# The out-projection of an mLSTM block as seven block products instead of eight

## The chip, the cores and the metric

One core of a Trainium2 chip runs one transformer block. The metric is the device time of one launch in microseconds; the kernel before takes 1096.12 us (median of three runs, 1095.81 to 1096.61). VectorE is called DVE in the rows, ScalarE ACT, GpSimd POOL, TensorE PE, and SyncE, which issues most transfers, SP.

## The reference, cut to what matters

```python
def mlstm_mixer(h, w_in, b_if, norm_w, w_out):
    ...
    hc = rms_norm(from_chunks(hc)).reshape(bsz, seq, ML_V_WIDTH) * norm_w.astype(f32)   # 4 heads of 256
    out = hc * jax.nn.sigmoid(o.astype(f32))
    return out.astype(h.dtype) @ w_out          # 1024 x 1024 by 1024 x 1024

        x = x + g1 * y                          # y: the mixer's output
        h = rms_norm(x) * (1.0 + sc2) + sh2
        x = x + g2 * swiglu(h, ffn_w_gate_up[layer], ffn_w_down[layer])
```

Everything is float32. The change is in `out @ w_out`, in the adding of it to x, and in the second norm behind it.

## The kernel before, in words

The 1024 tokens are eight tiles of 128. Every float32 product is made of three products of a rounded part (H) and a residue (L): HH, HL, LH. So an operand is first rounded by ScalarE into hH or wH, and VectorE subtracts that from the source into hL or wL. Order between engines is by semaphores; each engine works its own queue in the order in which the code is written.

**Heads.** `head(h)` runs four times. For each of eight chunks c TensorE does `scores`, a projection of 24 matmuls and `attend(h, c - 1)`. VectorE does `weighted`, `value_low`, `state` (the matrix C, which `attend` reads), `divide`, `gating`, `weighted_low`, and in between two `ada_item` (the sums of the modulation rows, both operands in SBUF; SP loads one item for each, `ada_item` in the sync queue). GpSimd makes qs (qT times sI) for the next `attend`, and hg, the gated head output, 128x256 per head and chunk, row of tile t in `hg[:, t, :]`. In head 3 it also scales the first out-projection weights by the gate g1 (`scale_unit`, L714).

**Out-projection.** w_out comes in four units of 256 columns; g1 is multiplied in by GpSimd in the raw buffer, ScalarE rounds (`split_H`), VectorE takes the residue (`split_L`, L1289). There is one raw buffer of two halves: `load_unit` (L427) loads a half only when the residue of the half before it has been taken. Rows of hg are normed per head: `head_root` (L942, ScalarE) takes the root for four tiles of all heads, `head_rstd` the reciprocal, `head_norm` (L723 on GpSimd, L1423 on VectorE) multiplies a whole row tile of 128x1024. TensorE transposes each tile (`out_transposes`, L2098, two banks of PSUM); `og_high` (L948) rounds it out of PSUM into hH and `og_low` (L1430) takes the residue out of PSUM into hL. `y_tile(n)` on TensorE (L2223) makes 24 matmuls, eight K tiles times three, of 512 columns (two units) or 256; on VectorE (L1612) it adds the bank to x in x2. Tiles go over the first two units, then the last; the order is in `y_sequence` (L60).

**End of the stage.** `Y_SECOND` finishes one row tile after the other in the order of TOKENS. For each finished tile ScalarE squares and roots it (`row_square`, L1104), VectorE takes the reciprocal (`row_inverse`), scales it into xs (`norm_row`, L1846), TensorE transposes it in two halves into three banks (`transposes2`, L2009), ScalarE and VectorE copy one half each with the modulation (`copy_rows`, L1073 and L1854), ScalarE and VectorE split it (`high`, `low`, L1331). On VectorE the order in each step is add, residues of an earlier tile, copy, and only then reciprocal and `norm_row`. GpSimd makes sums of halves of x2 (T1 to T4) for the up products, which are already made as 2x2 block products with seven multiplications; `up_product(n, q)` (L2267) waits for the operand of its q in all tiles. The first of them are (0, 2), (0, 1), (1, 2), (1, 1), and then (0, 5), the first that reads T1.

## Time and profile before

| | |
|---|---|
| median of the runs | 1096.12 us |
| profiled execution, first to last instruction (span) | 1095.6 us |
| its own time as a run | not listed apart; the runs lie within 1095.81 to 1096.61 |
| TensorE, VectorE, ScalarE, GpSimd busy | 98%, 67%, 41%, 14% |
| TensorE's granted clock | 0.999 over the span |
| out-projection, first product to first up product | 355.87 to 459.58 us |

The span is 0.5 us under the median. Busy time is the time in which an engine executes; a row's "us" for a group of several instructions reaches from the first start to the last end. Successive instructions overlap in the rows by about a tenth of a microsecond, so the pitch (start to start) is shorter than the duration. "<-" behind idle time names what ended it.

### The profile page before, as it was taken

To read this page: it belongs to the slowest core of one execution; us is meant where nothing else is said; L and a number is where in the kernel's file an instruction comes from. 1 tells how busy PE (TensorE), PEld (TensorE's weight loads), DVE (VectorE), ACT (ScalarE), POOL (GpSimd) and SP (SyncE) were. 2 spreads that over 40 slices of the span, in tenths; PEclk is the share of its full clock that TensorE was granted. 3 is DMA by queue.
4 is the path that set the end of the run, shared out by engine and by line. 5 is a ranking of instruction groups with operands and counts; after the bars stand their busy time and mean duration, and the time that the engine had idled before them with its cause. 6 is when DMAs were issued, how large, how long until landed. Compare 5 with 4: busy or idle time off the path is not lost.

```text
span 1095.6 us, 14969 instructions
## 1 busy us (share of the span) xinstructions
PE 1077.3 (98%) x5290; PEld 910.4 (83%) x5290; DVE 729.4 (67%) x1285; ACT 450.8 (41%) x826; POOL 157.4 (14%) x145
## 2 busy tenths in 40 slices
PE   6999999999999999999999999999999999999997
PEld 6899888888888897888888888888888888888886
DVE  6867757477479636888767566766766465844676
ACT  7862322232224316664433343333333325544444
POOL 3732312212326412410000000000000000000000
PEclk9999999999999999999999999999999999999999
DMA  9425532432531523115555526444552889655643
GB/s 377 167 80 169 185 109 87 140 114 61 160 114 58 193 78 116 78 39 172 159 169 166 184 93 221 145 142 156 177 187 91 289 281 396 231 193 184 200 154 154
DMA packets 86970, 177.11 MB, mean 162 GB/s; under 512 B 8152, under 2 KB 31320, under 8 KB 85872
## 3 DMA queue, kind: packets, MB, share of 16 engines
q1 hardware_dynamic: 85984, 174.80, 47.1%
q0 software_dynamic: 480, 1.09, 0.4%
q8 instruction: 42, 0.69, 0.3%
q10 hardware_dynamic: 432, 0.27, 0.1%
q14 instruction: 32, 0.26, 0.1%
HBM read 135.97 MB, written 40.16 MB: 161 GB/s over the span
## 4 chain that ended last, share of the span: by engine, by line
PE 95%; DVE 2%; DMA 1%; ACT 1%; issue 1%; POOL 0%; DVEq 0%; POOLq 0%; SPq 0%
PE OP L2263 27%; PE OP L1994 19%; PE O L2263 15%; PE ST L2263 5%; PE DC L2263 5%; PE AD L2263 5%; PE O L1994 4%; PE ST L1994 4%; PE AD L1994 2%; PE DC L1994 1%; PE O L2141 1%; PE ST L2042 1%; PE O L2157 1%; PE DC L2157 1%; PE O L2042 1%
## 5 line engine op out<-in xcount | busy, mean ns | idle before, releaser
L1994 PE MATMUL OP<-wH,hH 128*128 128x512 f32 (+1 forms) x400 | 142.1, 355 | 0.4 <-issue 0.4
L1994 PE MATMUL OP<-wH,hL 128*128 128x512 f32 (+1 forms) x400 | 139.1, 348 | 0.0
L1994 PE MATMUL OP<-wL,hH 128*128 128x512 f32 (+1 forms) x400 | 138.7, 347 | 0.0
L1759 DVE TENSOR_TENSOR dL<-dF,dH 128x1024 fp32r<-128x1024 f32 x77 | 93.0, 1223 | 68.6 <-ACT dH L1159 67.7
L1159 ACT CAST dH<-dF 128x1024 fp32r<-128x1024 f32 x77 | 79.9, 1052 | 88.0 <-DMA dF<-w_units 36.2
L2263 PE MATMUL OP<-tH,wsH 128*128 128x512 f32 x264 | 102.7, 389 | 0.0
L2263 PE MATMUL OP<-tH,wsL 128*128 128x512 f32 x264 | 102.7, 389 | 0.0
L2263 PE MATMUL OP<-tL,wsH 128*128 128x512 f32 x264 | 102.7, 389 | 0.0
L1994 PEld LDWEIGHTS OP<-wH,hL 128*128 128x128 f32 x400 | 75.6, 189 | 9.6
L1994 PEld LDWEIGHTS OP<-wH,hH 128*128 128x128 f32 x400 | 75.7, 189 | 9.3 <-issue 0.8
L1994 PEld LDWEIGHTS OP<-wL,hH 128*128 128x128 f32 x400 | 75.8, 190 | 8.6
L1071 ACT CAST wsH<-wsF 128x512 fp32r<-128x512 f32 x88 | 53.2, 620 | 49.6 <-DVE wsF L1675 42.8
L1071 ACT CAST wsH<-raw 128x512 fp32r<-128x512 f32 x66 | 38.8, 619 | 75.5 <-DMA raw<-w_units 61.8
L2263 PE MATMUL O<-hH,wsL 128*128 128x512 f32 x176 | 68.5, 389 | 0.0
L2263 PE MATMUL O<-hH,wsH 128*128 128x512 f32 x176 | 68.5, 389 | 0.0
L2263 PE MATMUL O<-hL,wsH 128*128 128x512 f32 x176 | 68.5, 389 | 0.0
L1714 DVE TENSOR_TENSOR wsL<-wsF,wsH 128x512 fp32r<-128x512 f32 x88 | 58.2, 686 | 14.4 <-ACT wsH L1071 14.4
L1670 DVE TENSOR_TENSOR wsF<-raw 128x512 f32<-128x512 f32 x21 | 14.5, 691 | 74.7 <-DMA raw<-w_units 65.2
L768 POOL TENSOR_TENSOR hg<-hc,gate 128x256 f32<-128x256 f32 x32 | 34.6, 1080 | 164.5 <-DVE gate L1518 164.5
L2263 PEld LDWEIGHTS OP<-tH,wsL 128*128 128x128 f32 x264 | 49.6, 188 | 10.3
L2263 PEld LDWEIGHTS OP<-tH,wsH 128*128 128x128 f32 x264 | 49.6, 188 | 10.3
L2263 PEld LDWEIGHTS OP<-tL,wsH 128*128 128x128 f32 x264 | 49.5, 188 | 10.2
(331 smaller groups left out, 2601.0 us busy)
## 6 DMA issues: line engine op xcount, KB each, us to landing
raw<-w_units SPq DMA_DIRECT2D x76, 512.0 KB, 4.6
dF<-act_mid SPq DMA_DIRECT2D x77, 256.0 KB, 2.7
ada<-ada_rest SPq DMA_DIRECT2D x64, 256.0 KB, 3.0
wst<-w_units SPq DMA_DIRECT2D x44, 256.0 KB, 5.0
down_mid<-wst SPq DMA_DIRECT2D x22, 512.0 KB, 3.2
dF<-down_mid SPq DMA_DIRECT2D x44, 256.0 KB, 3.0
dF<-w_units SPq DMA_DIRECT2D x33, 256.0 KB, 5.2
ada<-ada_first SPq DMA_DIRECT2D x8, 1024.0 KB, 10.0
```

What stands on the lines that cost most here:

```text
L768: nc.gpsimd.tensor_tensor(hg[:, c - 1, h * DV:(h + 1) * DV], hc[:, (c - 1) % 2, :], gate[:, (c - 1) % 2, :], ALU.mult).then_inc(hg_ok, 1)
L1071: nc.scalar.copy(wsH[n % 2][W_SLOT.index(q)][:], src).then_inc(c_H, 1)
L1159: nc.scalar.copy(dH[g][:], dF[g][:]).then_inc(d_H, 1)
L1670: nc.vector.tensor_tensor(f[5][:], gate_up_block(0, 1), gate_up_block(1, 1), ALU.add).then_inc(c_sum, 1)
L1714: nc.vector.tensor_tensor(wsL[n % 2][i][:], src, wsH[n % 2][i][:].bitcast(F32), ALU.subtract).then_inc(c_L, 1)
L1759: nc.vector.tensor_tensor(dL[g][:], dF[g][:], dH[g][:].bitcast(F32), ALU.subtract).then_inc(d_L, 1)
L1994: ins = nc.tensor.matmul(out_ap, lhs[a], rhs[b], start=(n == 0 and i == 0), stop=(last and i == 2))
L2042: ins = nc.tensor.matmul(XT_BANKS[2 * (t % 2) + j][:, k * P:(k + 1) * P], xin[:, t, (4 * j + k) * P:(4 * j + k + 1) * P], diag[:, t % 2, : ...
L2141: nc.tensor.matmul(O[c % 2][:, 0:width], qs[:, c % 2, :], C[:, 0:width], start=True, stop=False)
L2157: ins = nc.tensor.matmul(out_ap, lhs[a], rhs[b], start=(first and i == 0), stop=(i == 2))
L2263: ins = nc.tensor.matmul(out_ap, lhs[a], rhs[b], start=(first and i == 0), stop=(last and i == 2), skip_group_check=True)
```

## The change

w_out is cut into a 2x2 matrix of 512x512 blocks, and so is the normed, transposed activation (A11, A12 the first four token tiles with heads 0 and 1 and heads 2 and 3, A21 and A22 the last four). Seven products q of a sum of activation blocks (T1 to T4, A11, A12, A22) with a sum of weight blocks give the result; each product has four token tiles r of 12 matmuls of 512 columns. The partial products stay in PSUM banks and are added to x by VectorE after each product.

- **Weight sums** (`out_weights`): in heads 1 and 2 SP loads the four blocks of w_out in eight chunks into the part of hg that head 3 will fill, GpSimd scales each chunk by g1 and makes four sums, SP saves them to a buffer in DRAM (`out_mid`) and later loads them as units. The load of g1 moves from head 3 to head 1.
- **Norm**: `head_root(0)` covers heads 0 and 1 and runs in head 2; `head_root(1)` covers heads 2 and 3. `head_norm` does half a row (128x512): heads 0 and 1 by GpSimd in head 3's chunks 0 to 3; of heads 2 and 3 tiles 0 and 1 by VectorE, the rest by GpSimd.
- **Transposes**: 16 half tiles; five of them inside head 3. ScalarE copies each back into hg (`og_copy`), GpSimd sums blocks (`og_sums`, 16 of 128x512), ScalarE rounds and VectorE takes residues out of SBUF (`og_high`, `og_low`, 28 each).
- **Weights**: seven units; two of them and the unit for q = 4 are scaled by GpSimd, the others come scaled.
- **End of the stage**: twelve products in the order of `Y_ENDS`; TOKENS changes; a finished tile's reciprocal and `norm_row` follow its add at once on VectorE; the transposes use two banks, and those of the last two tiles run behind up products. The x loads of tiles 0 to 3 no longer wait for the last modulation row.

The diff, cut to its core:

```diff
@@ plans
-TOKENS = (0, 1, 4, 2, 5, 3, 6, 7)
+TOKENS = (0, 1, 2, 4, 3, 5, 6, 7)
+OUT_SEQ = (1, 2, 6, 7, 4, 5, 3)
+    ends = [(4, 0), (4, 1), (5, 0), (4, 2), (5, 1), (3, 0), (4, 3), (3, 1), (5, 2), (5, 3), (3, 2), (3, 3)]
+    ends = {2: row_tiles(0), 3: row_tiles(1), 5: row_tiles(2), 7: row_tiles(3), 8: row_tiles(4), 10: row_tiles(5)}
+    after = {0: row_tiles(6), 1: row_tiles(7)}
@@ banks
-        Y_BANKS = [OP[0], OP[1], DC, AD]
+        OUT_X = [OP[0], OP[1], DC, O[1]]
+        OUT_P2 = [O[0], AD]
+        OUT_Y = [O[0], AD, DC, O[0]]
-        TR_BANKS = [ST[0], ST[1], O[1]]
+        TR_BANKS = [ST[0], ST[1]]
@@ SP, in head(h)
+            load_at = {(1, 6): (0, 1), (1, 13): (2,), (1, 15): (3,), (2, 3): (4,), (2, 5): (5,), (2, 9): (6,), (2, 11): (7,)}
+            save_at = {(1, 12): 0, (1, 14): 1, (2, 2): 2, (2, 4): 3, (2, 8): 4, (2, 10): 5, (2, 14): 6}
...
                     ada_item(h, i, first)
+                    if (h, i) in save_at:
+                        save_out_chunk(save_at[h, i])
+                    for n in load_at.get((h, i), ()):
+                        load_out_chunk(n)
@@ GpSimd
+            def out_weights(n):
...
+                nc.gpsimd.tensor_tensor(bv, bv, gv, ALU.mult).then_inc(so_sum, 1)
+                pool.wait_ge(so_sum, 5 * n + 1)
+                nc.gpsimd.tensor_tensor(b22, b12, b22, ALU.add).then_inc(so_sum, 1)
...
+            chunk_at = {(1, 4): 0, (1, 5): 1, (1, 7): 2, (2, 0): 3, (2, 2): 4, (2, 3): 5, (2, 5): 6, (2, 6): 7}
...
+            for r in range(3):
+                og_sums("T1", r)
+            head_norm(1, 2)
+            head_norm(1, 3)
+            og_sums("T1", 3)
+            for t in range(4, NT):
+                head_norm(1, t)
+            for r in range(4):
+                og_sums("T2", r)
...
+            for r in range(4):
+                og_sums("T3", r)
+            scale_unit(U_OUT + 4)
+            for r in range(4):
+                og_sums("T4", r)
@@ VectorE, behind the heads
+            og_low("A11", 3)
             divide(NH - 1, NT - 1)
             gating(NH - 1, NT - 1)
-            og_low(1)
             split_acc(2 * NH - 1)
             split_L(U_OUT + 1, 1)
             head_rstd(1)
+            head_norm(0)
+            head_norm(1)
+            y_tile(1, 0)
...
+            y_tile(2, 3)
+            split_L(U_OUT + 3, 0)
+            og_low("T2", 3)
+            for r in range(4):
+                y_tile(6, r)
+                og_low("T3", r)
+            for r in range(4):
+                og_low("T1", r)
+            y_tile(7, 0)
+            split_L(U_OUT + 4, 1)
+            for r in range(1, 4):
+                y_tile(7, r)
+                og_low("T4", r - 1)
+            og_low("T4", 3)
+            split_L(U_OUT + 5, 2)
+            for r in range(4):
+                og_low("A22", r)
@@ VectorE, the last twelve products
+            finished = {Y_DONE[t] - 1 - N_Y1: p for p, t in enumerate(TOKENS)}
+            copies = {2: 0, 3: 1, 5: 2, 7: 3, 8: 4, 10: 5}
+            lows = {3: 2, 4: 3, 6: 4, 9: 6, 11: 7}
+            fill = {6: (2, 1), 7: (5,), 8: (7, 6), 9: (3, 4)}
+            for m, (q, r) in enumerate(Y_ENDS):
+                y_tile(q, r)
+                if m in finished:
+                    p = finished[m]
+                    row_inverse(NT + p, NT + TOKENS[p])
+                    norm_row(p)
+                if m == 2:
+                    split_L(U_OUT + 6, 0)
+                if m in copies:
+                    copy_rows(row_tiles(copies[m]))
+                if m in lows:
+                    low(HL_FIRST[lows[m]])
+                for i in fill.get(m, ()):
+                    up_low(0, i)
@@ TensorE
+            def out_product(q, r):
...
+                pe.wait_ge(og_L, OG_HL_AT[OUT_OPERAND[q], r] + 1)
...
+                for k in range(4):
+                    ins = chained(out_bank(q, r)[:], tuple(og_operand(h, kind, r)[:, k, :] for h in (hH, hL)),
...
+            attend(NH - 1, NT - 1)
+            out_product(1, 0)
+            out_transposes(7)
+            out_product(1, 1)
+            out_transposes(8)
+            out_product(1, 2)
```

## Rows read from the trace of the kernel before

**Rows 1.** the page: span, busy time of each engine, and the landing of a weight half

```profile
span 1095.6 us, 14969 instructions
...
PE 1077.3 (98%) x5290; PEld 910.4 (83%) x5290; DVE 729.4 (67%) x1285; ACT 450.8 (41%) x826; POOL 157.4 (14%) x145
...
raw<-w_units SPq DMA_DIRECT2D x76, 512.0 KB, 4.6
```

**Rows 2.** stretches: length; busy us of PE, PEld, DVE, ACT, POOL; clock, DMA share, GB/s

```profile
347.00:356.00 9.00, 7.85 (x46) 6.52 (x46) 8.65 (x20) 4.68 (x11) 7.50 (x6) 1.00 0.07 25
356.00:413.60 57.60, 56.45 (x339) 49.50 (x340) 28.00 (x42) 15.00 (x25) 19.66 (x12) 1.00 0.36 129
413.60:459.60 46.00, 44.80 (x250) 38.45 (x248) 34.67 (x70) 29.58 (x65) 14.81 (x11) 1.00 0.28 104
459.60:471.50 11.90, 11.90 (x60) 9.91 (x58) 10.66 (x17) 10.55 (x24) 3.68 (x3) 1.00 0.11 45
```

**Rows 3.** the chain of waits: start, us, engine, output, line, count

```profile
239.15 5.48 PE OP L1994 x24
246.10 5.47 PE OP L1994 x24
...
355.87 3.10 PE OP L1994 x24
...
471.65 2.72 PE O L2263 x12
```

**Rows 4.** TensorE's timeline: start, us, engine, line, operation, tiles, count

```profile
358.81 1.04 PE L2115 MATMUL ST<-ident,hg 128*128 128x128 f32 x8
```

**Rows 5.** VectorE's timeline, 355 to 366 us

```profile
364.35 0.24 DVE L1421 RECIPROCAL hrs<-hsd 128x16 f32<-128x16 f32 x1
```

**Rows 6.** groups of instructions by form, 355.8 to 459.5 us

```profile
L720 POOL TENSOR_TENSOR raw<-raw,gb 128x1024 f32<-128x1024 f32 x4 | 9.5, 2396 | 15.6 <-DMA raw<-w_units 15.6
...
L1289 DVE TENSOR_TENSOR wL<-raw,wH 128x1024 fp32r<-128x1024 f32 x6 | 7.1, 1219 | 0.0
...
L1865 DVE TENSOR_SCALAR x<-ST,mod 128x128 f32<-128x128 f32 x16 | 5.4, 399 | 0.0
...
L1619 DVE TENSOR_TENSOR x<-x,OP 128x512 f32<-128x512 f32 x6 | 4.1, 685 | 6.9 <-PE OP L1994 6.9
...
L821 POOL TENSOR_TENSOR x<-t,x 128x512 f32<-128x512 f32 x2 | 2.6, 1293 | 0.2
```

**Rows 7.** GpSimd's passes on hg: ns min/median/max, first and last start

```profile
L768 POOL TENSOR_TENSOR hg<-hc,gate x32: 725/742/1796, 90.0 to 357.3; 128x256 f32<-128x256 f32 x32
```

**Rows 8.** VectorE's timeline, 469 to 479 us

```profile
469.32 0.68 DVE L1331 TENSOR_TENSOR hL<-x,hH 128x512 fp32r<-128x512 f32 x1
...
471.65 1.78 DVE L1331 TENSOR_TENSOR hL<-x,hH 128x512 fp32r<-128x512 f32 x1
473.35 4.79 DVE L1331 TENSOR_TENSOR tL<-x,tH 128x512 fp32r<-128x512 f32 x6
```

**Rows 9.** GpSimd's timeline of the same stretch

```profile
469.49 1.69 POOL L821 TENSOR_TENSOR x<-t,x 128x512 f32<-128x512 f32 x1 [3.53 <-DVE t L1656]
471.14 3.45 POOL L824 TENSOR_TENSOR x<-x,t 128x512 f32<-128x512 f32 x2
```

**Rows 10.** one finished row, VectorE's timeline

```profile
428.13 1.29 DVE L1331 TENSOR_TENSOR hL<-x,hH 128x512 fp32r<-128x512 f32 x2
...
430.62 0.15 DVE L1720 RECIPROCAL rstd<-sd 128x1 f32<-128x1 f32 x1
430.80 0.75 DVE L1851 TENSOR_SCALAR xs<-x,rstd 128x1024 f32<-128x1024 f32 x1
```

**Rows 11.** the same row, ScalarE's timeline

```profile
429.43 0.29 ACT L1116 ACTIVATE sd<-ms,eps 128x1 f32<-128x1 f32 x1
```

**Rows 12.** an iteration of head 2, VectorE's timeline

```profile
247.32 0.47 DVE L1484 SCALAR_TENSOR_TENSOR C<-C,sI,DC 128x258 f32<-128x258 f32 x1
```

**Rows 13.** the same iteration, TensorE's timeline

```profile
251.87 0.60 PE L2141 MATMUL O<-C,qs 128*128 128x258 f32 x2
```

More of the change, by code:

```diff
@@ L44 @@
 U_FF = U_OUT + 4
+N_OUT = 7
+L_FF = U_OUT + N_OUT
 NU = U_FF + 3 * NG
@@ L57, with og_sequence, og_split @@
 STEPS = 7 * NG
+OUT_SEQ = (1, 2, 6, 7, 4, 5, 3)
+OUT_BLOCK = {1: (0, 0), 2: (1, 0), 4: (1, 1)}
+OUT_SUM = {6: 0, 3: 1, 7: 2, 5: 3}
+OUT_ADD = {1: (0, 0), 2: (0, 0), 6: (4, 0), 7: (4, 1), 4: (0, 1), 5: (4, 1), 3: (4, 0)}
 def y_sequence():
-    first = [(0, 1, 0), (0, 1, 1)] + [(0, 2, t) for t in range(2, 7)] + [(0, 1, 7)] + [(1, 1, t) for t in (0, 1, 7)]
-    second = [(2, 2, t) for t in TOKENS[:-1]] + [(2, 1, TOKENS[-1]), (3, 1, TOKENS[-1])]
-    return first, second
+    whole = [(q, r) for q in (1, 2, 6, 7) for r in range(4)]
+    ends = [(4, 0), (4, 1), (5, 0), (4, 2), (5, 1), (3, 0), (4, 3), (3, 1), (5, 2), (5, 3), (3, 2), (3, 3)]
+    return whole, ends
+def og_sequence():
+    return [(0, t) for t in range(NT)] + [(1, t) for t in range(NT)]
+def og_split():
+    seq = []
+    for kind in ("A11", "A12", "T2", "T3", "T1", "T4", "A22"):
+        seq += [(kind, r) for r in range(4)]
+    return seq
 def row_tiles(p):
@@ L593, in _ @@
             load_up(0)
-            save_rows(0)
-            save_rows(1)
+            for p in range(6):
+                save_rows(p)
             load_up(1)
-            for p in range(2, NT):
+            for p in range(6, NT):
                 save_rows(p)
@@ L750, in head @@
                 for c in range(NT + 1):
+                    if last and c == 1:
+                        pool.wait_ge(so_saved, 16 * 8)
                     if 1 <= c < NT:
@@ L835, in _ @@
             pool.wait_ge(c_L, 7 * NF)
[L836 removed]
+            to_all(g2b, 6, g_in)
         @block.scalar
@@ L1191, in _ @@
                 row_root(NT + p, NT + t)
-                copy_rows(TR_FIRST.get(p if p < NT - 1 else NT, ()))
-                if p == 3:
-                    up_cast(1, 2)
-                    up_cast(1, 1)
+                if p < 2:
+                    split_H(U_OUT + 6, 0, (y_mm, 16), (p,))
+                if 1 <= p < 7:
+                    copy_rows(row_tiles(p - 1))
+                for q in casts.get(p, ()):
+                    up_cast(0, q)
+            up_cast(1, 2)
+            up_cast(1, 1)
+            copy_rows(TR_AFTER[0])
             high(HL_AFTER[0])
@@ L1589, in head @@
                     weighted_low(h, c)
-                    if last and c == 6:
+                    if h == 2 and c == 6:
                         head_rstd(0)
+                    if last and c in (4, 5, 6):
+                        og_low("A11", c - 4)
                     if c in (1, 2):
@@ L1624, in _ @@
             head_rstd(1)
-            y_tile(0)
-            mod_row(2 * NH - 1)
-            for t in range(2, NT):
-                if t > 2:
-                    og_low(t)
-                y_tile(t - 1)
-                if t % 2 == 0 and t + 2 < NT:
-                    head_norm(t + 2)
-                if t == 5:
-                    split_L(U_OUT + 2, 2)
-            y_tile(NT - 1)
-            for n in range(NT, N_Y1):
-                y_tile(n)
-                if n == NT:
-                    split_L(U_OUT + 3, 0)
+            head_norm(0)
@@ new lines, in _ @@
+            head_norm(1)
+            y_tile(1, 0)
+            y_tile(1, 1)
+            og_low("A12", 0)
+            mod_row(2 * NH - 1)
+            y_tile(1, 2)
+            og_low("A12", 1)
+            y_tile(1, 3)
+            og_low("A12", 2)
+            og_low("A12", 3)
+            split_L(U_OUT + 2, 2)
+            y_tile(2, 0)
+            y_tile(2, 1)
+            og_low("T2", 0)
+            y_tile(2, 2)
+            og_low("T2", 1)
+            og_low("T2", 2)
+            y_tile(2, 3)
@@ L2216, in head @@
                         attend(h, c - 1)
+                    if h == NH - 1 and c in (1, 2, 3, 6, 7):
+                        out_transposes((1, 2, 3, 6, 7).index(c))
             first_head()
```

462 lines of the change are left out of this document (287 added, 175 removed).

## The prediction

> **What bounds the kernel now.** I read the page first: TensorE is busy 98% of the span, VectorE 67%, GpSimd 14% [rows 1]. So TensorE work that goes away is worth its whole price as long as nobody makes TensorE wait. Then the windows of the stage that changes [rows 2]: TensorE stands 1.15 us before the out-projection starts, 1.15 us in its first 57.6 us and 1.2 us in the next 46; VectorE is busy 28.0 of 57.6 us, then 34.7 of 46, then 10.7 of 11.9. The stage has air at its start and none at its end. The chain of waits fixes the clock of what follows [rows 3]: the out-projection starts at 355.87, 24 matmuls of 512 columns take 5.47 us, the first 24 of 256 take 3.10, and the first up product on operand T1, (0, 5), starts at 471.65. I use that last point as the finish line, since behind it the new kernel does what the old one does. Its T1 residue was ready at 470.0 (469.32 + 0.68) [rows 8], so VectorE is only 1.6 us ahead of TensorE there.
>
> **TensorE, removed.** Before: 12 tiles of 24 wide matmuls and 8 of 24 narrow ones, 12 x 5.47 + 8 x 2.87 (half a wide tile and a little; the row's 3.10 holds the start) = 88.6 us. After: 28 products of 12 wide matmuls, 28 x 2.73 = 76.4, or 2.72 as at the finish line. Gain 12.2 us. The transposes stay in number; eight cost 1.04 us at the most [rows 4], and five groups of four move into head 3, out of the stage. The ideal is 1096.1 - 12.2 = 1083.9.
>
> **What is added.** VectorE: 28 adds of 512 columns at a pitch of 0.60 for 12 wide and 8 half ones; 28 residues (og_low) instead of 16; seven weight units to split instead of four, each half 1.22 (1.15 from start to start, like the residues' 0.60 for 0.68) [rows 6, 10]. That is 16.8 - 10.0, 7.2 and 6.9: some 21 us. ScalarE: 16 copies out of PSUM, 12 casts and six weight halves, in a stage where it was busy 15.0 of 57.6 us; it stays off the path until the end of the stage. GpSimd: 16 sums of 128x512 at 1.29 (20.6 us) and, in heads 1 and 2, eight chunks of one 128x1024 scaling at 2.40 and four 128x256 sums at 0.74 [rows 6, 7]. The raw weight buffer has one reader chain: 4.6 us of DMA per half [rows 1], then cast, then residue.
>
> **What the two engines do to each other** is the core of this forecast. With GpSimd running two-operand passes, VectorE's 0.68 us residue takes 1.78 us; of the six behind it only the first waits, since GpSimd has ended by then (4.79 in all, 3.7 without a wait); GpSimd's 1.29 becomes 1.69 and 1.73 [rows 6, 8, 9]. Laid side by side, each pass starts when the other engine's ends: they alternate. An add whose second operand is in PSUM isn't held. By the Trainium skill (SBUF — State Buffer, "Who interferes with whom") a VectorE instruction with two SBUF inputs and a GpSimd instruction that reads SBUF exclude each other for a whole instruction; the trace agrees. Before, og_low read PSUM; now it reads the copy in SBUF, so all 28 residues, and every weight residue, must alternate with GpSimd. If they merely ran beside each other, step B below would cost about 0 and the sum would be some 7 us lower.
>
> I lay the new queues out in the old kernel's clock, TensorE starting product (1, 0) at 355.7.
>
> **A, the norm.** Before, head_rstd(1) ran at 364.35 [rows 5], some 8.7 us behind the last division, and TensorE needed it only at tile 4. Now it covers heads 2 and 3 of all rows, and out_transposes(8), behind two products only, needs it. Division, gate, squares, table load, root; on VectorE split_acc and both halves of split_L before the reciprocal, with T1 sums between: about 363.4. Then a half-width norm: 365.2. TensorE is there at 355.7 + 2 x 2.73 + 0.45 = 361.6 and stands 3.6 us. Old idle of the region was 2.3 us [rows 2].
>
> **B, T3 and T4.** TensorE reaches product (4, 0) at 407.5. It needs T4 row 0 and the unit U_OUT+4. From 388.4 (T2's last sum ended, its residue pending) GpSimd has eight sums and a scaling, 10.3 + 4.8 = 15.1 us, and VectorE, before it may split that unit, two weight halves and nine residues, 2.3 + 5.4 = 7.7. Both alternate on one port: 22.8 us, to 411.2. VectorE then does two adds, two weight halves, one residue, 4.1 us: (4, 0) starts at 415.4. TensorE stands 7.9 us.
>
> **C, the last twelve products.** VectorE finishes T4 and unit 5 at about 421.2 (its first half is loaded from 413.0 on, 4.6 us, then cast and split, then the second), then A22: 423.9, while (4, 0) has ended at 418.2. Its loop holds 12 adds (7.2), 8 finished rows, 6 copies of four at 0.33 (7.8), 2 weight halves (2.3), 14 row residues (8.4) and 7 up_low (4.2). A finished row now waits on the spot for ScalarE's square and root: 1.5 us from the add's end (0.08 behind 428.13) to the root's end (429.72), which before lay behind residues and copies: the reciprocal came at 430.62 [rows 10, 11]; with reciprocal and scaling 2.45 each, 19.6 in all. Sum 49.5 us against 38 us of TensorE (12 x 2.73 + 12 groups of transposes at 0.4). So VectorE ends it at 473.4 and TensorE has waited for it on the way, also because two transpose banks replace three. From there to T1's last residue: 7.9 us of sums, copies and residues, and 2 us for twelve GpSimd passes met on the way (0 to 8): 483. TensorE's (0, 5) starts 11.5 us later than 471.65.
>
> **D, heads 1 and 2.** A chunk is 2.4 + 4 x 0.74 plus four waits on itself, 6 us in an iteration of 6.95 (246.10 - 239.15) [rows 3, 7]. VectorE's ada sums read SBUF twice and alternate with it: 3 to 3.5 us late per chunk, 0.5 to 1.8 of idle to absorb it. TensorE reads the state C 4.1 us after VectorE has it (247.79 against 251.87) [rows 12, 13], so one late chunk is free and a pair of neighbours is not; qs queues behind the chunk too, and SP's save_out_chunk holds the next ada load. I take 3 us, between 0 and 8. The moved transposes, gate load and DMA bytes (8 MB in some 150 us) I cost at nothing: covered by TensorE's own work in head 3.
>
> **Sum.** 11.5 + 3 = 14.5; the TensorE gain of 12.2 is inside A to C. Span 1095.6 + 14.5 = 1110.1; the median of the runs is 0.5 over the span, so 1110.6. I say 1110. By the Trainium skill (GPSIMD Engine Reference, "Side-by-side cycle accounting") a 2048-column sum takes 4497 ns, an estimated 1.12 us for 512; the row says 1.29 [rows 6]. By the page's figure the eight sums in B would be 1.4 us shorter; I go by the row.
>
> **Rivals.**
> R1, faster: VectorE keeps up. Place: low T4 row 0 and unit 4 in front of (4, 0). If VectorE has both by 407.5, B is nil and the backlog into C small; it decides there, since C from 410 ends at 460, in front of the old kernel's own 459. For this GpSimd's passes would have to fall into VectorE's PSUM adds and waits. Price: 1083.9 + 1.5 (A net) + 0 to 4: 1085 to 1090. For it: VectorE is busy only 28.0 of the first 57.6 us. Against it: 22.8 us of demand in 19. 0.17.
> R2, eaten up: B is half, ScalarE's waits in C half covered by TensorE's own transposes, D nil: 12.2 gained, 4 + 8 lost, and a few us either way: 1092 to 1102. 0.18.
> R3, heads too: chunk pairs stall TensorE in each pair and the late ada loads hold VectorE: D is 8 or more, 1118 to 1128. 0.10.
> Main case, 1103 to 1118: 0.55.
>
> **The numbers.** Runs of this kernel lie within 0.07% of each other, so about 0.2% (2.2 us) can be told from no change. Slower: 0.55 + 0.10 + 0.07 of R2 = 0.72; same 0.06; faster 0.17 + 0.05 = 0.22. The range takes the main case, R2, and the upper part of R1: 1088 to 1118; the main case alone is 1103 to 1118.
>
> **What would show it.** TensorE idle before transposes of hg near 3.6 us; before product (4, 0) near 8 us with releaser VectorE (tL or wL); in the last twelve products near 11 us, released by xs and by VectorE's adds; og_low at a mean of 1.0 us or more instead of 0.68; VectorE over 9 of 10 us busy from 388 on. VectorE idle before rstd near 1.5 us, eight times. I am wrong if the residues stay near 0.7 us while GpSimd sums, or if TensorE is 98% busy in the stage.

## The result and the profile after

The changed kernel takes 1135.27 us (median of 4 runs, 1134.96 to 1135.79), the kernel before 1095.96 in the same comparison: a ratio of 1.0356, 95% interval 1.0344 to 1.0368. It is slower by 39.3 us. The forecast was 1110, with a range from 1088 to 1118; its sign was right and its size far too small: 14.5 us of growth against 39.3.

The head of the page of the changed kernel [rows 1]:

```profile
span 1133.7 us, 14957 instructions
...
PE 1078.3 (95%) x5146; PEld 903.9 (80%) x5146; DVE 778.3 (69%) x1311; ACT 472.7 (42%) x860; POOL 236.7 (21%) x207
...
raw<-w_units SPq DMA_DIRECT2D x74, 512.0 KB, 4.8
```

TensorE runs 144 matmuls fewer and is still busy 1.0 us longer. The 38.1 us of span come apart from this line alone: 12.2 us of matmuls are gone, so 1065.1 us would be left at the old pace; 1078.3 is 13.2 us over that; and the time in which TensorE is not busy grew from 18.3 us (1095.6 - 1077.3) to 55.4, by 37.1. -12.2 + 13.2 + 37.1 = 38.1. I put the 13.2 us down to matmuls at a lower granted clock, which the windows show [rows 2] (columns: length, then busy us of PE, PEld, DVE, ACT, POOL with counts, then clock, DMA share, GB/s). They go from head 3's end to product (1, 0), to product (4, 0), and to just before the finish line:

```profile
347.00:362.90 15.90, 15.34 (x85) 13.24 (x84) 15.17 (x36) 5.42 (x15) 8.24 (x7) 1.00 0.20 49
362.90:426.30 63.40, 52.52 (x232) 41.63 (x231) 52.74 (x51) 26.59 (x44) 43.03 (x28) 0.95 0.37 124
426.30:498.00 71.70, 51.61 (x228) 41.95 (x228) 47.27 (x86) 39.59 (x83) 16.05 (x12) 0.86 0.33 111
498.00:509.70 11.70, 8.27 (x29) 6.88 (x30) 11.43 (x18) 7.88 (x18) 3.74 (x3) 0.71 0.00 0
```

The finish line, the first up product on T1, starts at 509.7 instead of 471.65. Behind it the kernels take the same time (1133.7 - 509.7 = 624.0; 1095.6 - 471.65 = 623.95), so all of the loss lies in front of it. TensorE's longer waits there, from its timeline (start, us, instruction, count, and in brackets its idle time before and who ended it):

```profile
274.76 0.68 PE L2370 MATMUL O<-C,qs 128*128 128x258 f32 x2 [1.47 <-DVE PTL L1668]
282.70 0.67 PE L2370 MATMUL O<-C,qs 128*128 128x258 f32 x2 [1.08 <-DVE hc L1705]
337.14 0.40 PE L2325 MATMUL AD<-accH,oner 128*1 128x512 f32 x1 [1.71 <-ACT hg L1107]
372.29 0.66 PE L2344 MATMUL ST<-ident,hg 128*128 128x128 f32 x4 [3.28 <-DVE hg L1629]
390.71 0.47 PE L2457 MATMUL O<-wH,hH 128*128 128x512 f32 x1 [2.46 <-DVE x L1814]
406.13 0.50 PE L2457 MATMUL O<-wH,hH 128*128 128x512 f32 x1 [0.58 <-DVE hL L1634]
414.22 0.79 PE L2457 MATMUL OP<-wH,hH 128*128 128x512 f32 x1 [2.36 <-DVE hL L1634]
426.32 0.47 PE L2457 MATMUL OP<-wH,hH 128*128 128x512 f32 x1 [2.23 <-issue]
451.83 1.94 PE L2246 MATMUL ST<-ident,xs 128*128 128x128 f32 x8 [10.61 <-ACT x L1280]
476.49 1.09 PE L2246 MATMUL ST<-ident,xs 128*128 128x128 f32 x4 [6.26 <-DVE x L2083]
501.43 1.09 PE L2246 MATMUL ST<-ident,xs 128*128 128x128 f32 x4 [3.59 <-DVE x L2083]
```

In the kernel before no wait of TensorE in this stage is longer than 1.2 us, so the 10.61 us are new. The engine named, ScalarE, waited itself. Its timeline and VectorE's at that place:

```profile
450.19 1.50 ACT L1280 ACTIVATE x<-ST,mod 128x128 f32<-128x128 f32 x4 [9.81 <-DMA x_mid<-x]
```

```profile
440.93 2.36 DVE L1489 TENSOR_TENSOR wL<-raw,wH 128x1024 fp32r<-128x1024 f32 x2
450.21 1.37 DVE L2083 TENSOR_SCALAR x<-ST,mod 128x128 f32<-128x128 f32 x4 [6.92 <-DMA x_mid<-x]
```

Both may write over a row of x only when it has been saved to x_mid. SyncE's own timeline says why that was late:

```profile
442.18 1.47 SPq L621 DMA_DIRECT2D raw<-w_units  x2
443.69 0.91 SPq L631 DMA_DIRECT2D x_mid<-x  x2
```

The first row was normed at 437, but its save stands in SyncE's queue behind load_up(0), which waits for the residue of the seventh out unit. It went out at 443.69, and the two engines went on when it had landed, 6.5 us later. In the kernel before the same load went out at 404.12, ten us ahead of the first row's save (414.55), so nothing stood behind it. The order of the two in the queue is the same in both kernels; the change put three more units in front of what the load waits for, and all eight rows behind the same point.

### The profile page after: what moved, and what is told of

It is laid out like the page before. It is cut to its first block, busy times and chain, and to the rows that moved or that the text cites. A ratio compares the mean times of both kernels' runs of the same rounds, so it can differ in the third digit from the quotient of the medians.

```text
span 1133.7 us, 14957 instructions
## 1 busy us (share of the span) xinstructions
PE 1078.3 (95%) x5146; PEld 903.9 (80%) x5146; DVE 778.3 (69%) x1311; ACT 472.7 (42%) x860; POOL 236.7 (21%) x207
## 4 chain that ended last, share of the span: by engine, by line
PE 55%; DVE 0%; issue 0%; ACT 0%
PE OP L2457 25%; PE O L2457 15%; PE ST L2457 5%; PE AD L2457 5%; PE DC L2457 5%; DVE x L2083 0%; DVE wsL L1931 0%; PE ST L2246 0%; DVE x L2057 0%; DVE tL L1531 0%; DVE x L2028 0%; DVE sB L2026 0%; ACT sd L1312 0%; ACT junk L1370 0%; DVE rstd L1937 0%
## 5 line engine op out<-in xcount | busy, mean ns | idle before, releaser
L2220 PE MATMUL OP<-wH,hH 128*128 128x512 f32 (+1 forms) x320 | 113.8, 356 | 0.0
L2220 PE MATMUL OP<-wH,hL 128*128 128x512 f32 (+1 forms) x320 | 111.2, 348 | 0.0
L2220 PE MATMUL OP<-wL,hH 128*128 128x512 f32 (+1 forms) x320 | 111.0, 347 | 0.0
L1887 DVE TENSOR_TENSOR wsF<-raw 128x512 f32<-128x512 f32 x21 | 14.5, 691 | 78.7 <-DMA raw<-w_units 69.2
L1740 DVE SCALAR_TENSOR_TENSOR acc<-ada,cact,acc 128x512 f32<-128x512 f32 x56 | 56.5, 1010 | 17.0 <-DMA ada<-ada_rest 14.3
L2220 PEld LDWEIGHTS OP<-wH,hL 128*128 128x128 f32 x320 | 60.3, 189 | 7.7
L2220 PEld LDWEIGHTS OP<-wH,hH 128*128 128x128 f32 x320 | 60.4, 189 | 7.0 <-issue 0.2
L2220 PEld LDWEIGHTS OP<-wL,hH 128*128 128x128 f32 x320 | 60.5, 189 | 6.8
L1489 DVE TENSOR_TENSOR wL<-raw,wH 128x1024 fp32r<-128x1024 f32 x36 | 52.0, 1466 | 15.4 <-ACT wH L1005 15.3
L883 POOL TENSOR_TENSOR hg<-hc,gate 128x256 f32<-128x256 f32 x32 | 36.0, 1124 | 123.2 <-DVE gate L1718 123.2
## 6 DMA issues: line engine op xcount, KB each, us to landing
ada<-ada_first SPq DMA_DIRECT2D x8, 1024.0 KB, 10.2
```

The costliest lines, as they stand in the source:

```text
L883: nc.gpsimd.tensor_tensor(hg[:, c - 1, h * DV:(h + 1) * DV], hc[:, (c - 1) % 2, :], gate[:, (c - 1) % 2, :], ALU.mult).then_inc(hg_ok, 1)
L1489: nc.vector.tensor_tensor(piece(wL[:, slot(k), :], i), piece(raw, i), piece(wH[:, slot(k), :], i).bitcast(F32), ALU.subtract).then_inc(w_L, 1)
L1740: nc.vector.scalar_tensor_tensor(acc[:], ada[:, i % 2, :], cact[:, k:k + 1], acc[:], ALU.mult, ALU.add).then_inc(acc_ok, 1)
L1887: nc.vector.tensor_tensor(f[5][:], gate_up_block(0, 1), gate_up_block(1, 1), ALU.add).then_inc(c_sum, 1)
L2220: ins = nc.tensor.matmul(out_ap, lhs[a], rhs[b], start=(n == 0 and i == 0), stop=(last and i == 2))
```

## The experiments

All kernels are the changed one with edits: e1 to e4 and e16 carry only the edit named; e5 is e1 and e2 together; e6, e7 and e8 build on e5, e9 on e6, e10 on e9, e11 and e13 on e10, e12 on e11, e14 on e13 and e15 on e14. Each was timed in 3 rounds beside the kernel before on the same chip (its medians there: 1095.7 to 1096.4). "First row" is where TensorE starts the transposes of the first finished row tile (xs); "rest" is the span less that. "Head 2" is the stretch between the fifth and the sixth matmul AD<-accH,oner, that is the second half of head 2 (before: 251.41 to 296.55), the only stretch ahead of head 3 that got longer.

| kernel | median (runs), us | ratio, 95% interval | head 2 | first row | rest |
|---|---|---|---|---|---|
| before | 1096 | 1 | 45.14 | 420.37 | 675.2 |
| after | 1135.3 (1135.0-1135.8) | 1.0356 [1.0344, 1.0368] | 48.14 | 437.38 | 696.3 |
| e1 | 1128.1 (1126.9-1132.9) | 1.0298 [1.0275, 1.0322] | 48.23 | 438.77 | 692.3 |
| e2 | 1129.3 (1126.6-1131.7) | 1.0301 [1.0281, 1.0320] | 48.55 | 437.04 | 689.6 |
| e3 | 1123.5 (1122.5-1124.6) | 1.0248 [1.0233, 1.0263] | 48.37 | 426.87 | 695.9 |
| e4 | 1133.7 (1130.7-1136.2) | 1.0349 [1.0332, 1.0366] | 45.14 | 432.68 | 696.2 |
| e5 | 1122.1 (1121.5-1123.6) | 1.0237 [1.0222, 1.0252] | 48.33 | 437.39 | 683.0 |
| e6 | 1120.7 (1119.7-1121.2) | 1.0221 [1.0206, 1.0236] | 48.19 | 436.36 | 681.4 |
| e7 | 1107.2 (1104.6-1108.1) | 1.0102 [1.0085, 1.0119] | 45.14 | 420.38 | 682.4 |
| e8 | 1118.7 (1117.1-1120.2) | 1.0204 [1.0188, 1.0219] | 48.28 | 437.14 | 678.2 |
| e9 | 1110.6 (1109.8-1111.3) | 1.0133 [1.0116, 1.0150] | 48.19 | 427.08 | 681.9 |
| e10 | 1107.6 (1107.3-1108.2) | 1.0107 [1.0092, 1.0122] | 48.41 | 424.41 | 682.0 |
| e11 | 1108.8 (1108.5-1109.8) | 1.0120 [1.0103, 1.0137] | 50.04 | 425.46 | 681.2 |
| e12 | 1108.4 (1107.8-1109.7) | 1.0114 [1.0099, 1.0129] | 49.88 | 425.55 | 682.4 |
| e13 | 1106.4 (1103.7-1107.6) | 1.0090 [1.0067, 1.0113] | 46.58 | 421.93 | 682.4 |
| e14 | 1105.6 (1103.4-1106.2) | 1.0083 [1.0066, 1.0100] | 46.08 | 420.15 | 681.5 |
| e15 | 1106.0 (1104.6-1108.1) | 1.0093 [1.0076, 1.0109] | 46.26 | 421.75 | 683.2 |
| e16 | 1135.0 (1134.1-1136.0) | 1.0353 [1.0336, 1.0370] | 46.33 | 437.81 | 696.4 |

The start of the kernel, which no edit touches, moves by up to 1.9 us from run to run (that fifth matmul lies between 249.9 and 251.8), so differences of the stretches are worth more than absolute times. The stretches are of the one profiled run of each kernel; for e1 that was the slowest of its four (1132.9).

**The queue and the loop of the last twelve products: e1, e2, e5.** e1 moves two saves ahead of the load:

```diff
-            load_up(0)
-            for p in range(6):
+            for p in range(2):
+                save_rows(p)
+            load_up(0)
+            for p in range(2, 6):
                 save_rows(p)
```

> The changed kernel with one thing moved on SyncE's queue: the first two saves of finished rows (x_mid) stand ahead of the load of the first up-weight unit, whose wait is for the residues of the seventh out unit (ended at 443.3 in the changed kernel). Theory (queue): the two 9.8-us and 6.9-us waits of ScalarE's and VectorE's row copies on x_mid<-x go, and with them TensorE's idle stretch of 10.6 us at 451.8; a part comes back later, since VectorE's loop is behind it: 1124 to 1129 us, the finish line (first up product) at 499 to 504 instead of 509.7. Rival (VectorE is the bound of the last twelve products anyway): the idle stretch only spreads out over the later rows, a gain under 3 us, 1132 to 1135.

e2 moves a finished row's inverse and norm, on VectorE, behind the copies and residues of its step:

```diff
                 y_tile(q, r)
-                if m in finished:
-                    p = finished[m]
-                    row_inverse(NT + p, NT + TOKENS[p])
-                    norm_row(p)
...
                 for i in fill.get(m, ()):
                     up_low(0, i)
+                if m in finished:
+                    p = finished[m]
+                    row_inverse(NT + p, NT + TOKENS[p])
+                    norm_row(p)
```

> The changed kernel with row_inverse and norm_row at the end of each step of the last twelve products instead of ahead of the step's copies and residues, so that VectorE has other work while ScalarE makes the root. Theory of the prediction (the loop of VectorE, waits of 1.5 us on ScalarE's root in each row, sets the length of the stage): 3 to 8 us less, 1127 to 1132. Rival (SyncE's queue holds the first rows until 450 whatever VectorE does): within 2 us of the changed kernel's 1135; it may get longer, as the row norms come later.

> The two moves of the runs before in one kernel: the first two row saves ahead of the load of the up weights, and the inverse and norm of a row at the end of each step. Each alone took about 7 and 6 us off the changed kernel's 1135.3. Theory (two separate losses: SyncE's queue holds the first rows, VectorE's waits on the root hold the later ones): the gains add up, 1120 to 1124, and from the first of the last twelve products to the first up product it takes 66 to 72 us instead of 83.4. Rival (the one loss covers the other): no better than the better of the two, 1126 to 1129.

e1: 7.2 us less by the medians, 4.0 in "rest". The wait of 10.61 us is gone from its timeline, but what follows it shows that VectorE was next:

```profile
446.10 1.09 PE L2248 MATMUL ST<-ident,xs 128*128 128x128 f32 x4 [2.17 <-DVE x L2085]
...
473.46 1.09 PE L2248 MATMUL ST<-ident,xs 128*128 128x128 f32 x4 [6.84 <-DVE x L2085]
```

The windows from (4, 0) to the finish line, changed kernel first, then e1:

```profile
426.30:509.70 83.40, 59.88 (x257) 48.83 (x258) 58.70 (x103) 47.46 (x101) 19.79 (x15) 0.84 0.28 96
```

```profile
427.60:506.80 79.20, 61.67 (x257) 49.63 (x258) 62.21 (x103) 47.55 (x101) 21.03 (x15) 0.83 0.29 101
```

TensorE stands 17.5 us there instead of 23.5: of the 10.6 us, 4.6 came back as other waits for VectorE's loop, in which each row stands at least 1.54 us at the root. The same matmuls took 1.8 us longer, so the stretch is 4.2 us shorter. e2 is the mirror image: 5.9 us less by the medians, with SyncE's 9.99 us still there. Both together (e5): 13.2 us by the medians, as much as the sum of the two (13.1), 13.3 in "rest", and 69.8 us from (4, 0) to the finish line instead of 83.4: inside the theory's bounds, and the rival falls. The waits of VectorE in this stretch (who for whom, total us, times, longest), changed kernel first, then e5:

```profile
DVE rstd L1937 <- ACT sd L1312: 15.7, 8, 3.4
DVE x L2083 <- DMA x_mid<-x: 6.9, 1, 6.9
```

```profile
DVE rstd L1939 <- ACT sd L1314: 3.6, 4, 1.5
```

e1's time lies in its theory's range (1128.1 for 1124 to 1129), but its finish line does not: 506.8 for 499 to 504. e2's lies in its own (1129.3 for 1127 to 1132), and its rival, within 2 us, falls.

**What bounds the loop then: e6 and e8.** e6 gives rows 1, 3 and 5 the banks OP[0] and OP[1]:

```diff
         TR_BANKS = [ST[0], ST[1]]
+        TR_ROW = [TR_BANKS, OP, TR_BANKS, OP, TR_BANKS, OP, TR_BANKS, TR_BANKS]
...
-                    if e >= 2:
+                    if e >= 14:
                         pe.wait_ge(*copied(e - 2))
+                    elif e >= 4:
+                        pe.wait_ge(*copied(e - 4))
+                    elif e >= 2:
+                        pe.wait_ge(y_ev, Y_AT[4, 1] + 1)
```

> The kernel e5_saves_norm with four banks instead of two for the transposes of the row tiles: rows 1, 3 and 5 use the two OP banks, which the product (4,0) and (4,1) leave free. Theory (TensorE, in order, waits for a bank because VectorE's copy of the row before is late, and the products behind are held by that): 4 to 8 us below e5_saves_norm, the waits of the transposes on VectorE's row copies shrink to under 2 us together. Rival (VectorE's work itself is the bound of this stretch; a bank more only moves the wait to its norms or residues): within 1.5 us of e5_saves_norm.

> The kernel e5_saves_norm with the twelve residues of the row tiles (hL<-x,hH, kinds Q11, Q21, Q22) that VectorE makes between the last twelve products cut to 2 of 128 columns in each of four blocks; the numbers of the up products are not the reference's. Theory (VectorE's busy time is the bound of this stretch): each of the twelve passes is 0.5 to 0.6 us shorter, and where they alternate with GpSimd's more, so 6 to 9 us below e5_saves_norm. Rival (the round trips row by row, root, norm, transpose, copy, are the bound, not the busy time): under 2 us.

e6 gained 1.3 us: the rival's case, a bank more only moves the wait to xs. e8 gained 3.4 us for some 6.6 us of VectorE time taken away (twelve passes by 0.55): neither theory's number. VectorE was busy 51.45 us of the 58.3 between (4, 0) and 484.7 in e5 while TensorE had 50.28 us of work there; it is the fullest engine, and the round trips through ScalarE cost beside it. "Rest" stays at 681 to 683 in every kernel that builds on e5 but e8, 6 to 8 us above before's: this is the part that I could not remove. A likely reason, which no run tests by itself: in the kernel before eight rows were finished over tiles of 5.5 us each; seven products finish nothing until the last twelve, so VectorE's rows, copies and residues meet in one place. TensorE's clock is part of it too: from (4, 0) to the finish line these kernels were granted 0.88 to 0.93.

**The sums: e3, e7, e9.** e3 and e7 cut passes; e9 moves the sixteen operand sums to VectorE's own order, one line of it:

```diff
             y_tile(2, 1)
+            og_sums("T2", 1)
             og_low("T2", 0)
```

> The changed kernel with twelve of the sixteen operand sums of the out-projection (T1, T3, T4) made over 8 of their 512 columns; the semaphores stay, the numbers of three products are not the reference's. Theory (GpSimd's passes of two SBUF operands alternate with VectorE's and make both late between the products (1,0) and (4,0)): the 63.4 us between these two fall to 54 to 57, TensorE's idle stretches of 2.4, 2.3 and 2.2 us there shrink to under 3 us together, and the time is 1127 to 1130. Rival (the stage behind it, held by the row saves behind the load of the up weights, sets the end): the products before start earlier but the finish line moves by under 3 us, since the load still waits for the last out unit's residues, which also come earlier then by what the products gain.

> The kernel e5_saves_norm with both kinds of sums cut to 8 columns: GpSimd's scaling and sums of the out weights in heads 1 and 2, and T1, T3 and T4 of the operand sums; the numbers of the products they feed are not the reference's. Theory (these are losses of their own in other stages): the gains of 12 and 3 us, read from the traces of the two runs before, add to e5_saves_norm's, 1105 to 1109. Rival (the last twelve products wait for something with a fixed place, and take back what comes earlier): 1112 or more.

> The kernel e6_four_banks with all sixteen operand sums of the out-projection made by VectorE instead of GpSimd, each placed in VectorE's order where its inputs are ready. Theory (a GpSimd pass of two SBUF operands holds VectorE's next such pass until it ends, which costs VectorE more than the 0.68 us of the pass itself: 5.9 us for one residue at 408 while GpSimd scales a weight unit and begins T4): 5 to 9 us below e6_four_banks, and no VectorE residue of the stage over 3.5 us except beside the scaling. Rival (VectorE is the fullest engine of the stage, and sixteen passes more cost it 9.6 us): within 1.5 us of e6_four_banks, or slower.

e3 took 11.8 us off by the medians, more than expected (1123.5 for 1127 to 1130), and the 63.4 us became 53.0; "first row" came 10.5 us earlier and "rest" stayed at 695.9. The rival, that the stage behind would swallow it, falls. e7 lies 14.8 us below e5, of which 3.2 are in head 2, within its bounds.

e9 is the finding of this study: with the same sixteen passes on the engine that is fullest anyway, the time falls by 10.2 us (5 to 9 were expected), nearly as much as e3 took off by cutting twelve of them. No residue there takes over 2.4 us. The residues and weight residues on VectorE between (1, 0) and (4, 0), grouped by form (count, busy us, mean ns, idle before), in the changed kernel and in e9:

```profile
L1634 DVE TENSOR_TENSOR hL<-hg,hH 128x512 fp32r<-128x512 f32 x13 | 19.0, 1482 | 3.9 <-ACT hH L1120 3.9
L1489 DVE TENSOR_TENSOR wL<-raw,wH 128x1024 fp32r<-128x1024 f32 x8 | 14.3, 1822 | 0.0
```

```profile
L1600 DVE TENSOR_TENSOR hL<-hg,hH 128x512 fp32r<-128x512 f32 x13 | 11.1, 869 | 1.8 <-ACT hH L1086 1.8
L1455 DVE TENSOR_TENSOR wL<-raw,wH 128x1024 fp32r<-128x1024 f32 x8 | 9.4, 1216 | 0.2 <-ACT wH L971 0.2
```

The sixteen sums took VectorE 13.7 us in e9, 0.68 to 1.23 on the mean by kind (GpSimd's norms and one scaling still stand beside them). On GpSimd they took 28.0 us in the changed kernel, 1.5 to 2.0 on the mean, where an undisturbed one takes 1.29 [rows 6], and VectorE's next residue was held meanwhile. Busy time in the stretch fell on both engines: 52.74 us of 63.4 to 49.13 of 53.9 on VectorE, 43.03 to 18.58 on GpSimd. The windows of e9 for (1, 0) to (4, 0) and from there to the last row:

```profile
362.20:416.10 53.90, 49.20 (x232) 39.54 (x231) 49.13 (x67) 26.62 (x44) 18.58 (x12) 1.00 0.43 146
416.10:473.40 57.30, 47.73 (x224) 37.92 (x224) 51.14 (x86) 39.43 (x83) 17.70 (x12) 0.97 0.40 140
```

The same 232 matmul records took 52.52 us in the changed kernel at a clock of 0.95 and 49.20 here at 1.00: 3.3 us of that stretch were clock, not waiting.

**Head 3: e10.** ScalarE's copy out of the AD bank goes ahead of its wait for the value projection:

```diff
                     nc.scalar.copy(PTH[:, c % 2, :], PT[:, c % 2, :]).then_inc(pt_H, 1)
+                    if last and c in (2, 3, 4, 7):
+                        r = min(c - 2, 3)
+                        og_copy(r)
+                        og_high("A11", r)
                     act.wait_ge(v_mm, h * NT + c + 1)
```

> The kernel e9_vector_sums with ScalarE's copies of the transposed rows out of the AD bank in head 3 moved ahead of its wait for the next value projection, into the 4.2 us that it stands idle there. Theory (TensorE's four short waits in head 3, 0.56, 0.56, 1.71 and 0.56 us, are for this copy of the one AD bank): these waits go and the time is 2.5 to 3.5 us below e9_vector_sums. Rival (VectorE's loop in head 3 has no slack either, so it takes the time back): under 1 us.

2.95 us less by the medians; all four waits are gone, and the next stretch between two AD<-accH,oner matmuls, in head 3, is 33.87 us instead of 37.23 (before 32.53; two of the five transposes lie behind it). The theory holds.

**Head 2: e4, e11, e13, e15, e16.** e4 narrows the views that GpSimd's five passes of a chunk work on (the scaling likewise, in a line of its own):

```diff
-                b11, b21, b12, b22 = (b[:, u, :] for u in range(4))
+                b11, b21, b12, b22 = (b[:, u, 0:8] for u in range(4))
```

> The changed kernel with GpSimd's out-weight scaling and sums in heads 1 and 2 made over 8 of their 256 columns; the weight sums are then not the reference's. Theory (these passes make VectorE's passes late and TensorE waits 1.5 and 1.1 us in heads 1 and 2): head 3 starts 2.5 to 3 us earlier and the time is 1132 to 1133. Rival (the five transposes and the extra instructions, not the port, make the heads longer): head 3's start moves under 0.7 us, 1135.

e4: the stretch is 45.14 us, to the hundredth that of before, so GpSimd's chunks cause all 3.0 us; how, it doesn't say. The median fell by 1.5 us only, so 1133.7 misses the theory's 1132 to 1133, and its runs spread over 5.5 us; the last section shows what can move a time so.

In the trace qs ended just before TensorE's two waits did, so e11 makes it first:

```diff
                     if (h, c) in chunk_at:
+                        if c < NT - 1:
+                            make_qs(c + 1)
```

> The kernel e10_early_copy with GpSimd's qs for the next chunk made ahead of the scaling and sums of an out-weight chunk in heads 1 and 2 instead of behind them. The out-weight work stays the same. Theory (TensorE's two waits in head 2, 1.58 and 1.21 us, are for qs, which stands behind 6.5 us of out-weight passes in GpSimd's own order, not for VectorE's passes made slow beside GpSimd): both waits go and the time is 2 to 3 us below e10_early_copy. Rival (the prediction's: VectorE's passes beside GpSimd's are late): the waits stay, under 0.7 us.

That reading fell: the stretch got 1.6 us longer and the time 1.2. e11's VectorE timeline showed another suspect:

```profile
278.73 0.75 DVE L1711 SCALAR_TENSOR_TENSOR acc<-ada,cact,acc 128x512 f32<-128x512 f32 x1 [4.87 <-DMA ada<-ada_rest]
...
281.73 0.47 DVE L1655 SCALAR_TENSOR_TENSOR C<-C,sI,DC 128x258 f32<-128x258 f32 x1
```

The state update C stands behind an ada pass that waits for its load, and the load stands behind a save in SyncE's queue. The queue's own longest wait in the changed kernel, 251 to 300 (total, times, longest), is for GpSimd's sums, ahead of a save:

```profile
SPq L557 <- POOL hg L834: 15.7, 3, 7.2
```

e13 moves two saves and the loads behind them one item on (in save_at chunk 4 from (2, 8) to (2, 9) and 5 from (2, 10) to (2, 11); in load_at 6 from (2, 9) to (2, 10) and 7 from (2, 11) to (2, 12)):

> The kernel e10_early_copy with SyncE's saves of the out-weight chunks 4 and 5 in head 2, and the loads behind them, one ada item later in SyncE's queue. All passes stay. Theory (the 3 us of heads 1 and 2 come from SyncE's queue: a save waits for GpSimd's sums, and the ada load behind it lands 2 us after VectorE wants it, with C and PTL behind that on VectorE): VectorE's wait for ada goes, TensorE's two waits of 1.6 and 1.2 us go, and the time is 2 to 3 us below e10_early_copy. Rival (VectorE's passes are slow beside GpSimd's): both waits stay and the time is within 0.7 us of it.

The stretch fell from 48.41 to 46.58 us and the 1.6-us wait went, but not the one of 1.2 us nor VectorE's waits for ada, and the median fell by 1.3 us, between theory and rival. Chunk 6's save still stood ahead of the last ada load, so e15 moves it too (from (2, 14) to (2, 15), on e14), and e16 makes all three moves on the changed kernel alone.

> The kernel e14_t4_first with the save of out-weight chunk 6 one ada item later too, behind the load of the last ada item of head 2. Theory (SyncE's queue): in e13_late_saves this ada load still stood behind the save of chunk 6, issued at 271.6, and VectorE waited 2.4 us for it; with it moved the second half of head 2 falls from 46.1 to between 45.1 and 45.4 us, as before the change. Rival (what is left there, about 1 us, is the port): the stretch stays at 45.9 or more.

> The changed kernel as it is, with only the saves of chunks 4, 5 and 6 and the two loads behind them later in SyncE's queue. Theory (the whole of the 3 us of head 2 is SyncE's queue, though GpSimd's passes are all there): the stretch from the fifth to the sixth bias row is 45.1 to 45.6 us instead of 48.14, and the time 2 to 3 us below the changed kernel's 1135.3. Rival (queue and port share it): 46.0 to 47.0.

46.26 and 46.33 us: both rivals, not my theory. The move of chunk 6 gained nothing: e14, without it, has 46.08, and e13, with the same code in head 2 as e14, 46.58, so half a us in this stretch can't be told from none. The moves in SyncE's queue took away 1.8 of the 3.0 us of head 2 (e13, e16). What is left, 1.1 to 1.2 us with GpSimd's passes there and nothing with them cut (e4), fits the port (VectorE's eight passes on ada took 10.6 us in e16 and 6.6 before), but that was not tested by itself, and VectorE still waited 2.6 us for its ada loads in e16, so a part of it may be the queue's too. And e16's median is 0.2 us below the changed kernel's, where 2 to 3 were expected: in the profiled run, won in head 2 and lost behind it. The last section shows where.

**Two that gained little: e12, e14.**

> The kernel e11_qs_first with the square, root, inverse and norm of the last row tile ahead of the residues and casts of the step before it, on ScalarE and VectorE. Theory (TensorE's 4.61-us wait for xs behind the first up product comes from the place of this norm behind five residues that wait for GpSimd's t): 2 to 5 us below e11_qs_first. Rival (the residues are needed just as soon by the up products): under 1 us either way.

> The kernel e13_late_saves with the casts and residues of T4 ahead of those of T1 on ScalarE and VectorE, and the weight unit of T4's product split ahead of them. Theory (product (4, 0) waits 2.2 us for T4's first residue, which stands behind four T1 residues that are needed four products later): that wait goes and the time is 1 to 2.2 us less. Rival (VectorE is the bound through the last twelve products too, so that what is gained at (4, 0) is waited for at the first finished row): under 0.7 us.

e12: 0.5 us, inside the spread, as its rival said. The wait at that place fell from 4.63 to 3.01 us, now for ScalarE's copy, and the next one rose from 1.45 to 3.21. e14: 0.8 us by the medians, not to be told from none; the 2.28-us wait before (4, 0) turned up as 1.93 us before (5, 0), for the next weight residue. e14 is the fastest version, 1105.6 us, and still 9.6 us slower than the kernel before; none of the sixteen beat the kernel before (e15 is e14's equal).

## Why the prediction was right in sign and wrong in size

The sum was 14.5 us; the span grew by 38.1, that is 23.6 more. By its own marks: product (1, 0) came at 362.9 for a forecast 358.7 (355.7 + 3), then 63.4 us to (4, 0) for 59.7, then 83.4 to (0, 5) for 67.6: 4.2, 3.7 and 15.8. Sorted by cause, 13.2 of the 23.6 us are the clock, which the sum did not have; 6 are waits behind SyncE's queue in C; the other 4 are mostly the moved transposes in head 3. The clock's share rests on the rows; the other two have runs of their own (e1 and e5, e10).

- **D, heads 1 and 2** (3 us, measured 3.0). Right in size, and partly by luck: the sum priced the alternation alone, "SP's save_out_chunk holds the next ada load" stood there unpriced beside it, and e13 and e16 show that it was the larger part (1.8).
- **"The moved transposes, gate load and DMA bytes (8 MB in some 150 us) I cost at nothing: covered by TensorE's own work in head 3"** failed. It is TensorE's own order that they stand in: five transposes, and 3.4 us of waits for the one AD bank (0.55, 0.56, 1.71, 0.56), since ScalarE copies it out only behind 4.2 us of waiting for something else. With a start that was 0.4 us later (1, 0) came 4.2 us behind its mark; e10 took 2.95 back.
- **A, the norm** (3.6 us, measured 3.28 and then e3 and e9, without T1's sums on GpSimd, under 0.5). Right, with the cause: T1's sums between the norm passes, since e3 changes nothing but sums.
- **B** (7.9 us of waiting at (4, 0)). The waits came to 7.6 us, in four pieces (2.46, 0.58, 2.36, 2.23) instead of one: right in sum, wrong in place. Of the 3.7 us missing 3.3 are clock. "VectorE over 9 of 10 us busy from 388 on" came true only from 398 on (27.8 of 28.3 us).
- **C** (VectorE's loop of 49.5 us, finish 67.6 behind (4, 0)) is the step that failed most, by 15.8 us. Two terms are missing from it. The larger is the clock: "12 x 2.73 + 12 groups of transposes at 0.4" took every matmul at the full clock. With the four up products ahead of (0, 5) the stretch has 16 products and 16 groups of transposes, an estimated 50.1 us at these prices, and TensorE was busy 59.9: 9.8 us, at a granted clock of 0.84. The other is SyncE's queue: "Its loop holds 12 adds, 8 finished rows, ..." counted VectorE's passes and its waits for ScalarE's root and left out who else holds a finished row. The reordering puts row saves behind a load that waits for the last out unit; that is 10.6 us in one piece, and TensorE stood 23.5 us in all where 67.6 - 50.1 leaves 17.5. I had followed SyncE's queue for the chunk saves and not here. With the saves moved (e1) TensorE stood those 17.5 us, and what was left over the forecast, 79.2 for 67.6, was clock. The root waits came to 15.7 us: 1.54 in five rows, as forecast, and 2.10, 2.53 and 3.39 in the others. That e5 comes near the forecast (69.8 for 67.6) doesn't bear C out: e5 has taken away most of the root waits, which C counts.
- **The span and the time.** The sum adds 0.5 us between the two. The changed kernel's profiled run took 1135.55 us for a span of 1133.7, so the two differ by 1.85, and the 0.5 compared two executions. That is 1.4 us, too little to matter here.
- **The rivals.** "Keeps up" and "eaten up" fell with the time itself, and e3, e5 and e9 show why: the sums on GpSimd, the root and the queue each have a price. "Heads too" came nearest in total (1118 to 1128), by the wrong road: its D of 8 or more was 3.0.
- **What the port does.** The alternation was the core of the forecast and the runs carry it: residues at a mean of 1.48 us with the sums on GpSimd, 0.87 with them gone from it (e9). The Trainium skill (SBUF — State Buffer, "Who interferes with whom") calls it an exclusive lock; e9 agrees (1.48 against 0.87 us), and shows the use of that rule which I missed: here a short pass was cheaper on the engine that it would otherwise hold up.

## What to carry to other kernels

When a change adds work in front of a wait in a DMA-issuing queue, read everything behind that wait in the queue, even lines that the diff doesn't touch: two losses here were of that kind (a wait of 10.6 us, worth 7.2 by e1's median, and 1.8 us of head 2), and neither showed as a busy engine. Put a price on the clock too: where a forecast has TensorE waiting several times, its matmuls behind the waits may be slower, and that was the largest term that mine lacked. Don't hand a short two-operand SBUF pass to GpSimd to relieve VectorE in a stretch where VectorE makes such passes; count what it holds up (here sixteen passes moved back gave 10 us). And a scheme that does less arithmetic but finishes all its outputs in its last products wants the engines behind it idle there; in none of these kernels did the 12 us of matmuls saved pay for it.

## What the runs showed of the hardware that was not expected

**A lower clock behind short waits.** The kernel before is granted 1.00 in every window of the stage. In the changed one TensorE comes out of the 3.28-us wait at 372.29, out of the 10.61-us one, and out of others, at the lower of its two levels (1.2 GHz of 2.4) for a few us. The same followed the wait of 2.36 us at 414.22, but not the one of 2.46 us at 390.71. Its timeline behind the first of these, then behind the one at 414.22:

```profile
373.53 0.63 PE L2457 MATMUL DC<-wH,hL 128*128 128x512 f32 x1
373.96 0.63 PE L2457 MATMUL DC<-wH,hH 128*128 128x512 f32 x1
...
376.09 0.50 PE L2457 MATMUL DC<-wH,hL 128*128 128x512 f32 x1
```

```profile
414.81 0.63 PE L2457 MATMUL OP<-wL,hH 128*128 128x512 f32 x1
415.24 0.63 PE L2457 MATMUL OP<-wH,hL 128*128 128x512 f32 x1
```

From start to start that is 0.43 us, where the same matmul takes 0.23 elsewhere. Over the kernel it adds up to 13.2 us of TensorE time; in e5, e10 and e7 to 11.2, 5.8 and 4.7 (busy 1076.3, 1070.9, 1069.8, less 1065.1). Against the growth of idle time (37.1 us; 25.8, 17.2 and 14.7 in the three others) that is 0.32 to 0.43: a wait of TensorE cost its own length here and three or four tenths more. No run changed the clock alone; that part rests on the rows.

**One residue was held over two of GpSimd's passes.** The residue that the changed kernel starts at 408.29 takes 5.87 us, over the end of one GpSimd sum and both halves of a scaling, and ends where the next sum has begun:

```profile
408.29 5.87 DVE L1634 TENSOR_TENSOR hL<-hg,hH 128x512 fp32r<-128x512 f32 x1
```

```profile
408.89 4.70 POOL L815 TENSOR_TENSOR raw<-raw,gb 128x1024 f32<-128x1024 f32 x2
413.56 6.83 POOL L919 TENSOR_TENSOR hg<-hg,og 128x512 f32<-128x512 f32 x4
```

Each pass waiting for one of the other's, as the forecast laid it out, is the mean picture and not a rule: here VectorE waited for two. What decides that is open.

**Two lengths of one stretch.** From the transposes behind the 3.28-us wait to product (4, 0) the work is the same in all kernels that leave GpSimd's operand sums alone, but it took 54.0 us in the changed kernel (372.29 to 426.32) and in e2 (371.91 to 425.92), 53.8 to 54.1 in e4, e5, e6 and e8, and 56.8 in e1 and e16, whose edits lie elsewhere. The windows of the changed kernel and of e16:

```profile
372.29:426.32 54.03, 46.40 (x202) 36.92 (x203) 43.75 (x40) 21.99 (x34) 35.05 (x23) 0.94 0.29 95
```

```profile
369.77:426.52 56.75, 47.68 (x202) 37.93 (x203) 43.15 (x40) 22.01 (x34) 35.12 (x23) 0.92 0.27 89
```

In e16 all twelve matmuls of the product behind that wait ran at the lower level, in the changed kernel the first nine. Of the 2.7 us TensorE was busy 1.3 longer and stood 1.4 longer; what sets off the longer form is not shown. This is where e16's 1.8 us went in its profiled run. From run to run the clock goes along with the time in e1, whose four lie in the order of their mean granted clock (1126.9 us at 0.988, 1127.4 at 0.987, 1128.8 at 0.986, 1132.9 at 0.982), but not everywhere: e16's fastest, 1134.1 us, had its lowest, 0.980. A kernel with such waits has a time that can move by 2 to 3 us in a stretch that no edit touched; stretches between fixed points told more here than medians did.
